# A hybrid S5, attention and mixture-of-experts layer: the beginning ordered by landings, and the attention's roots, rows and outputs moved

## What is computed

```
sh_m, sc_m, g_m, sh_f, sc_f, g_f = split(silu(c) @ w_mod + b_mod, 6)       # and the same with c_ctx
z = (rms_norm(x, g) * (1 + sc_m) + sh_m) @ w_in                            # 2208 columns
mixed = concat(s5(z0), diff_attention(q, k, v), mla(cq, ckv, kr))
x = x + g_m * (mixed @ w_out)
x = x + g_f * moe(modulate(rms_norm(x), sh_f, sc_f))                       # 32 experts, 2 of them per token
# differential attention, 4 heads of 128:
lam = exp(sum(l0 * l1)) - exp(sum(l2 * l3)) + lam_init
p = softmax(q1 k1) - lam * softmax(q2 k2);  o = rms_norm(p @ v, g) * (1 - lam_init)
```

## Time and profile before

| | |
|---|---|
| median of 3 runs | 958.68 us (957.24 to 961.83) |
| the profiled execution's own time | 957.51 us |
| its span, first to last instruction | 955.6 us |
| granted TensorE clock, mean | 0.962 |
| TensorE busy | 866.6 us, 91% |
| VectorE, ScalarE, GpSimd busy | 446.8, 248.4, 134.9 us |
| read from HBM | 264.61 MB |

### The profile page before, as it was taken

The page is one execution under the profiler, slowest core; times in us unless marked ns, Lnnn a source line. Parts: engine busy times, 40 slices in busy tenths (PEclk is TensorE's granted clock), DMA queues, the critical chain, the costliest instruction groups (busy, mean ns, idle before and its releaser), DMA issues.

```text
span 955.6 us, 12764 instructions
## 1 busy us (share of the span) xinstructions
PE 866.6 (91%) x4433; PEld 438.0 (46%) x4433; DVE 446.8 (47%) x1126; ACT 248.4 (26%) x569; POOL 134.9 (14%) x364
## 2 busy tenths in 40 slices
PE   4999999999989989999999999999999976867895
PEld 1675546554445555546534444444444433333232
DVE  4596888769688646025862222222132322212127
ACT  4701023202467564113221111202021211111112
POOL 1311001020100000000011221212121222212110
PEclk9999999999999999999999999999999989787998
DMA  8962203535920373033979999999999999999985
GB/s 338 371 183 37 88 1 113 119 109 218 392 53 1 110 247 128 27 150 144 385 303 385 418 420 418 419 420 420 421 421 418 420 418 418 419 418 418 418 353 227
DMA packets 56374, 267.25 MB, mean 280 GB/s; under 512 B 10838, under 2 KB 17294, under 8 KB 29457
## 3 DMA queue, kind: packets, MB, share of 16 engines
q1 hardware_dynamic: 44432, 249.71, 65.0%
q0 software_dynamic: 11728, 16.99, 6.6%
q10 hardware_dynamic: 176, 0.05, 0.0%
HBM read 264.61 MB, written 25.17 MB: 303 GB/s over the span
## 4 chain that ended last, share of the span: by engine, by line
PE 46%; issue 23%; SPq 11%; DMA 10%; DVE 4%; POOL 3%; ACT 2%; POOLq 1%; ACTq 0%; DVEq 0%
PE PS L803 14%; SPq L413 8%; DMA BIG<-in_moe_w 7%; PE PS L1053 6%; PE PS L984 5%; DMA BIG<-in_w_mod 3%; PE PS L991 2%; PE PS L727 2%; PE PS L1022 2%; POOL held L618 1%; PE PS L1031 1%; SPq L418 1%; POOL BIG L627 1%; PE PS L672 1%; PE PS L1252 1%
## 5 line engine op out<-in xcount | busy, mean ns | idle before, releaser
L803 PE MATMUL PS<-BIG 128*128 128x512 f32 (+2 forms) x352 | 139.5, 553 | 0.0
L803 PEld LDWEIGHTS PS<-BIG 128*128 128x128 f32 x352 | 64.2, 190 | 65.9 <-issue 65.3
L1255 PE MATMUL PS<-S5Z,QKV 128*128 128x512 f32 x192 | 83.4, 592 | 0.0
L1280 PE MATMUL PS<-BIG,GM 128*64 128x512 f32 x320 | 73.6, 601 | 1.5 <-DMA BIG<-in_moe_w 1.5
L1244 PE MATMUL PS<-BIG,QKV 128*32 128x256 f32 x768 | 51.8, 423 | 19.6 <-DMA BIG<-in_moe_w 19.6
L618 POOL TENSOR_TENSOR held<-held 1x1 f32<-1x1 f32 x141 | 25.8, 183 | 301.6 <-PE PS L1228 182.7
L2552 DVE TENSOR_TENSOR QKV<-PS,QKV 64x512 f32<-64x512 f32 x48 | 33.0, 688 | 65.2 <-PE PS L1280 41.0
L1252 PE MATMUL PS<-BIG,QKV 128*64 128x512 f32 x256 | 58.7, 609 | 2.5 <-DMA BIG<-in_moe_w 2.5
L1053 PE MATMUL PS<-BIG 128*128 128x512 f32 x128 | 56.0, 594 | 0.0
L1255 PEld LDWEIGHTS PS<-S5Z,QKV 128*128 128x128 f32 x192 | 36.1, 190 | 43.0 <-issue 43.0
L1633 ACT ACTIVATE QKV<-PS,fcp 128x128 f32<-128x128 f32 x120 | 45.1, 456 | 35.1 <-PE PS L1228 35.1
(11 more groups left out here) (557 smaller groups left out, 1237.3 us busy)
## 6 DMA issues: line engine op xcount, KB each, us to landing
BIG<-in_moe_w SPq DMA_DIRECT2D x84, 1024.0 KB
BIG<-in_moe_w SPq DMA_DIRECT2D x21, 2048.0 KB
S5Z<-in_moe_w SPq DMA_DIRECT2D x40, 1024.0 KB
BIG<-in_w_mod SPq DMA_DIRECT2D x11, 2048.0 KB, 7.6
S5Z<-in_moe_w SPq DMA_DIRECT2D x10, 2048.0 KB, 24.3
BIG<-in_w_in SPq DMA_DIRECT2D x3, 2048.0 KB, 17.7
QKV<-in_x SPq DMA_DIRECT2D x8, 512.0 KB, 10.1
BIG<-in_w_out SPq DMA_DIRECT2D x2, 2048.0 KB, 17.4
```

Source lines behind the costliest of these rows:

```text
L803: ins = mm(dst[:, c0:width], hT[:, k, tok], wslot(n, width)[:, k, c0:width], start=(k == 0), stop=(k == KD - 1))
L1255: ins = mm(bank(2 + m), hgT[:, k, :], w13(side)[:, m, k, :], start=(k == 0), stop=(k == KD - 1))
L1280: ins = mm(PS[64 * n:64 * n + 64, 2560:3072], hidT[:, k % 2, 64 * (k // 2):64 * (k // 2) + 64], w2s(side)[:, k, 512 * n:512 * (n + 1)], st ...
```

## The change

- SP no longer loads c and c_ctx; ScalarE's queue does, ahead of b_mod.
- w_mod's block ("mod", 0, 3) is loaded as two DMAs of 128 rows with a semaphore each; `mod_rows` takes the halves to multiply. The first half's products stand before the tokens' turns, the second's behind. The warm-up products change from 4, 2, 1, 5 to 2, 2, 1, 2 and stand elsewhere.
- Tiles 0 and 1 are modulated slice by slice, each slice signalled by itself, and the first `project_u` takes the slices in the order 0, 4, 1, 5, ... as they come. ScalarE's Sqrt (which loads the table) stands behind `mod_copy(0, 6)`.
- Lambda is computed on two rows instead of 128; a TensorE product with ones spreads the difference.
- `mod_rows(2, 3, 7)`, its turn, copy and columns move into the first blocks of the attention.
- In block 15 ScalarE copies before it takes the exponentials of block 16; head 3's `head_out` goes to block 19, before that block's copy and behind the exponentials of block 20.
- The root of the heads' sums: VectorE makes a first guess by bit operations, and GpSimd three steps of refinement (12 operations on 128x16) that give the inverse root directly. ScalarE's Sqrt and VectorE's reciprocal go.
- `out_part(0, ...)` is split: slice 0 in block 29, slice 1 in block 30, the others in block 31; output 0 uses bank 7.

```diff
+SEED = 0x5F3759DF + (7 << 22)
-        lamr = S5R[:, 0:4 * DHD]
+        lamr = S5R[0:2, 0:2 * DHD]
+        root = S5R[:, 7168 + DH * NLT:7168 + 2 * DH * NLT].bitcast(I32)
+        norm = S5R[:, 7168 + DH * NLT:7168 + 2 * DH * NLT]
+        hT_n = lambda tiles: tiles + 3
+        op_bank = lambda i: 7 if i == 0 else i % 4
...
# SP
-            sp.dma_start(rows[R_C:R_C + 8], a["c"][0].rearrange("(r e) -> r e", e=P)).then_inc(sem("c_in"), 16)
-            sp.dma_start(rows[R_CC:R_CC + 8], a["c_ctx"].rearrange("(r e) -> r e", e=P)).then_inc(sem("c_in"), 16)
+                    if slot_of[n] == RING:
+                        for kk in range(2):
+                            sp.dma_start(mslot(n)[:, kk], src[P * kk:P * (kk + 1)]).then_inc(sem(f"mod_last{kk}"), 16)
+                        continue
# GpSimd
+            pool.wait_ge(sem("ssq"), 1)
+            for again in range(3):
+                st(pool.tensor_tensor(root_tmp, norm, norm, ALU.mult))
+                st.settle()
+                st(pool.tensor_tensor(root_tmp, root_tmp, ssq, ALU.mult))
+                st.settle()
+                st(pool.tensor_scalar(root_tmp, root_tmp, -0.5, 1.5, ALU.mult, ALU.add))
+                st.settle()
+                ins = pool.tensor_tensor(norm, norm, root_tmp, ALU.mult)
...
+            ins.then_inc(sem("rms"), 1)
# TensorE
             mod_rows(0, 0, 6)
+            pe.wait_ge(sem("consts"), 2)
+            warm(2, 1)
...
             mod_rows(0, 1, 6)
-            warm(4, 1)
+            warm(2, 1)
             mod_rows(0, 2, 6)
+            mod_rows(0, 3, 6, (0,))
             for t in range(NCT):
                 turn_tokens(t)
-            warm(2, 1)
-            mod_rows(0, 3, 6)
+            pe.wait_ge(sem("lam"), 3)
+            mm(bank(1, 1, 400), ones[0:2, :], sml[0:2, 492:493], start=True, stop=True).then_inc(sem("lam"), 1)
+            mod_rows(0, 3, 6, (1,))
             warm(1, 1)
             turn_mod(0, 7)
-            warm(5, 1)
+            warm(2, 1)
...
-                for k in range(KD):
+                for k in (0, 4, 1, 5, 2, 6, 3, 7):
+                    if (c, h) == (0, 0):
+                        half, kk = "ad"[k // 4], k % 4
+                        pe.wait_ge(sem(f"hT_{half}"), kk + 1 if kk < 3 else hT_n(NCT))
...
-            mod_rows(2, 3, 7)
             project_latent("nv", 2)
-            turn_mod(2, 7)
...
             for u in range(3):
                 scores(u)
+            mod_rows(2, 3, 7)
...
                 turn_first(b)
+                if b == 1:
+                    turn_mod(2, 7)
...
+                    if t == 0:
+                        pe.wait_ge(sem("b7_free"), len(b7_order))
+                        ring_wait(at[("out", 0)])
+                    if t < 2:
+                        out_part(0, (t,))
                     pe.wait_ge(sem("pt_out"), turned_n(b - 1))
                     pair_values(NHD - 1, slice(t * P, (t + 1) * P))
                 if b == len(blocks) - 1:
-                    out_part(0, range(KD - 1))
+                    out_part(0, range(2, KD - 1))
# ScalarE
+            small(rows[R_C:R_C + 8], vec(a["c"][0], 8), "c_in")
+            small(rows[R_CC:R_CC + 8], vec(a["c_ctx"], 8), "c_in")
             small(rows[R_BMOD:R_BMOD + 48], vec(a["b_mod"][0], 48), "rows_in")
...
+            mod_copy(0, 6)
             A(silu_t[:, 0:1], epsb[:, :], ACT.Sqrt)
-            mod_copy(0, 6)
             act.wait_ge(sem("gmc"), 1)
-            modulated(0)
-            modulated(1)
+            act.wait_ge(sem("xh_tr"), NCT)
+            for k in range(4):
+                for t in range(NCT):
+                    ins = A(hT[:, k, t * P:(t + 1) * P], bank(2 + 2 * t, P, k * P), ACT.Identity,
+                            scale=gmc[:, k, 1:2], bias=modc[:, 8 * M_SH + k, 1:2])
...
-                probs(first_u(b + 1))
+                if b + 1 < NBD:
+                    probs(first_u(b + 1))
+                if b == 0:
+                    mod_copy(2, 7)
                 probs_out(b, 512 * 6, range(4), 2 * b + 1)
+                if b + 1 == NBD:
+                    probs(first_u(b + 1))
...
+                if b - 1 in heads_out and b > NBD:
+                    head_out(heads_out[b - 1])
                 probs_out(b, 512 * 4, range(NT), turned_n(b))
-                if b in heads_out:
-                    head_out(heads_out[b])
-                if b == RMS_AT:
-                    act.wait_ge(sem("ssq"), DH)
-                    A(ssq, ssq, ACT.Sqrt, scale=1.0 / P).then_inc(sem("rms"), 1)
# VectorE
+                if h == DH - 1:
+                    st(ts(root, ssq.bitcast(I32), 1, None, ALU.logical_shift_right))
+                    st(ts(ssq, ssq, 1.0 / P, None, ALU.mult))
+                    st.settle()
+                    ts(root, root, -1.0, float(SEED), ALU.mult, ALU.add).then_inc(sem("ssq"), 1)
...
+                if b == 2:
+                    mod_cols(2, (8, 4), 7, "modc")
...
                 if b == DIAG_AT:
                     dve.wait_ge(sem("rms"), 1)
-                    st(V.reciprocal(ssq, ssq))
```

More of the change, by code:

```diff
@@ L662, in ring_wait, with mod_rows @@
                 pe.wait_ge(sem(f"ring_in{slot_of[n]}"), 16 * sum(slot_of[m] == slot_of[n] for m in range(n + 1)))
-            def mod_rows(g, r, b):
+            def mod_rows(g, r, b, halves=(0, 1)):
                 n = at[("mod", g, r)]
-                ring_wait(n)
-                for kk in range(2):
+                if slot_of[n] != RING:
+                    ring_wait(n)
+                for kk in halves:
                     k = 2 * r + kk
+                    if slot_of[n] == RING:
+                        pe.wait_ge(sem(f"mod_last{kk}"), 16)
                     for j in range(4):
@@ L1846, in _ @@
             dve.wait_ge(sem("gmc"), 1)
-            modulated(0)
-            modulated(1)
+            dve.wait_ge(sem("xh_tr"), NCT)
+            for k in range(4, KD):
+                for t in range(NCT):
+                    ins = ts(hT[:, k, t * P:(t + 1) * P], bank(3 + 2 * t, P, (k - 4) * P),
+                             gmc[:, k, 1:2], modc[:, 8 * M_SH + k, 1:2], ALU.mult, ALU.add)
+                    if k == KD - 1:
+                        ins.then_inc(sem("hT_d"), 1)
+                if k < KD - 1:
+                    ins.then_inc(sem("hT_d"), 1)
             normed(2)
```

67 lines of the change are left out of this document (35 added, 32 removed).

## The result

| | before | changed |
|---|---|---|
| median | 957.96 us (956.59 to 961.83, 4 runs) | 947.21 us (941.78 to 953.16, 4 runs) |
| profiled execution's own time, span | 957.51, 955.6 us | 950.38, 948.3 us |
| granted TensorE clock, mean | 0.962 | 0.966 |
| TensorE busy | 866.6 us | 860.1 us |

A forecast was written before the change was run, and what follows sets the result against it. Bound by TensorE's chain, then from about 500 us by the expert weights' DMA stream. Terms of 2.0, 0.45, 2.2, 5.4 and 0.9 us sum to 10.95, giving 946.6 profiled and 947.8 against the 958.68 median; range 943.5 to 954.0.

The forecast's parts named there:

- beginning: First 60 us: earlier w_mod landings, halved fourth block and slice-wise first projection; gain 2.0 us, bounds 0.2 and 2.6.
- adaLN rows: First attention blocks: moving mod_rows(2,3) behind the third score brings the first turned block 0.45 us earlier; bounds 0 and 1.2.
- block 15: Attention block 15: copying first removes TensorE's 1.12 us wait and keeps the clock; gain 2.2 us, bounds 1.0 and 2.2.
- head 3's copy, roots: Attention blocks 19 to 24: copy's wait, table loads and half clock go; 5.4 us together, 6.3 with fast roots, 4.5 slow.
- out-projection pieces: Last attention blocks: one 0.9 us piece fills one of TensorE's copy waits; gain 0.9 us, bounds 0 and 0.9.
- rival B: Half clock returns in the attention, losing 3.5 us at the roots or 1.1 in block 15; about 951.3 us; chance 0.15.
- What is saved ahead of about 500 us moves the end by as much: Whole kernel: savings on the chain before the full-rate expert weight stream reach the end in full, 10.95 us in sum.
- Rival A: Beginning: c lands late under w_mod's stream, row loads 3 to 4 us later; gain falls to 0.2, 949.6 us; chance 0.15.
- Rival C: Roots: GpSimd's chain beyond 3.3 us after the hand-over holds VectorE; about 960 us at 1.5 us a step; chance 0.02.
- Rival D: Attention savings meet an expert weight load not yet there; only 2 to 3 us pass to the end, 956 us; chance 0.05.
- what the profile after was to show: Signs: first projection near 32, first score about 255.5, turned block 2.5 us earlier, full clock 323 to 365, out-projection near 437.

The follow-up runs named there:

- lam_wide: Changed kernel plus an unused broadcast load of lambda to 128 rows at the old place in GpSimd's queue; 949.09 us, ratio 0.9898.
- c_on_sp: Changed kernel with c and c_ctx loaded by SP ahead of w_mod again; 947.76 us, ratio 0.9899.
- copy_back: Changed kernel with head 3's copy and square behind block 18's own copies again, roots left on GpSimd; 947.15 us, ratio 0.9895.
- block15_back: Changed kernel with block 16's exponentials ahead of block 15's copies again; 950.48 us, ratio 0.9916.
- roots_back: Changed kernel with the square root on ScalarE and the reciprocal on VectorE again, head 3's copy left as changed; 949.42 us, ratio 0.9901.
- begin_only: Kernel before with only the beginning's part of the change, lambda on two rows included; 955.69 us, ratio 0.9972.
- attn_only: Changed kernel with the beginning of the kernel before, attention kept as changed; 951.16 us, ratio 0.9915.
- rows_in_gap: Changed kernel with the product mod_rows(2, 3, 7) alone moved directly behind the last latent projection; 947.17 us, ratio 0.9891.
- rows_back: Changed kernel with mod_rows(2, 3, 7), its turn, copy and columns ahead of the attention again; 946.37 us, ratio 0.9872.

## Why the prediction was right, point by point

| term | predicted | in the profiles | 
|---|---|---|
| beginning | 2.0 | 3.4 |
| adaLN rows | 0.45 | -2.2 |
| block 15 | 2.2 | 3.0 |
| head 3's copy, roots | 5.4 | 7.2 |
| out-projection pieces | 0.9 | 0.9 |
| sum at the out-projection's end | 10.95 | 12.3 |
| between there and the logits' end | 0 | -3.7 |
| between there and the end of the span | 0 | -1.4 |
| sum at the end of the profiled execution | 10.95 | 7.2 |

The time was right (947.8 forecast, 947.21 measured), partly by terms that cancel. That it came within 0.6 us is luck: the four runs span 11.4 us, and all ten runs of the changed kernel have a median of 949.06. For the profiled execution the same sum gave 946.6, and it took 950.38. The two timings of the change gave 10.7 and 8.6 us.

- **Beginning**: the mechanism was right, the size was off. "The 128-fold broadcast of lambda becomes two rows; I count nothing for it" is the step: lam_wide puts it at 1.8 us. What is left, 1.6 us, stands against my 2.0 for c's queue, the halves and the slices; c's queue is 0.5 of it by the third block's start in c_on_sp (0.8 forecast). The four warm-up products that I counted as missing before the third block are not: eight stand ahead of it in both kernels, four of them now ahead of the second.
- **adaLN rows**: this step failed. It said that TensorE "goes on at 260.4 + 1.9 = 262.3", all at full clock, and took 0 as the lower bound. At full clock the move is worth 1.1 us (copy_back); the profile gave back 3.3 us by half clock, which the prediction had put at nothing here, its rival B looking for it only in the later blocks. I had read that the first score comes earlier, and not that taking the product away leaves TensorE idle in the place where it stood, 2.29 us. The product put into the gap avoids this in two of two profiles.
- **Block 15**: 3.0 us, by block15_back 1.3 for the wait and 1.7 for the half clock, against 1.1 and 1.1. A stretch of 3.4 us costs 1.7, half of its length, and I had counted only two scores' stretching.
- **Copy and roots**: GpSimd's twelve steps took 4.1 us (4.6 forecast), VectorE waited 1.00 (1.3 forecast). The parts: 1.2 us for the copy (copy_back; 0.5 forecast), 2.6 for the roots at full clock (roots_back), and 3.4 for the half-clock stretch of 6.8 us that stood in the profile of before. The twelve profiles with at least one of the two edits have no half clock between squares 3 and the pair; the two with neither (before, begin_only) have it, for 6.8 and 3.4 us. With each edit taken back alone the clock stayed full, in one profile each, so each may be enough by itself; why is open.
- **Out-projection pieces**: 0.9, as forecast (from the pair to the out-projection's end 84.10 us for 84.96).
- **"What is saved ahead of about 500 us moves the end by as much"**: true of transfers, as the 413 GB/s from 500 to 930 show, but not of the stretch from 437 to 453. In the profiled run 3.7 us went there, and 1.9 more by the first product of L1296. (The digits of the earlier trace rows turn to 9 for good only in the 22nd slice, from about 502 us; the 21st is a 7.) This is no property of the change: begin_only, whose attention is the old one, has it too, and the kernel before had none under its logits but a stretch at 457 to 460. Of twelve profiles without the added products seven have logits of 12.4 us or more behind the out-projection, five 9.1 to 9.6; of two with them none has.
- **Rival A** (949.6): c came at 6.95 and the first silu_c at 8.02, as it said, and the loss did not follow, as c_on_sp shows: TensorE has to wait for the first w_mod block too, in the changed kernel until 8.66. The Trainium skill, DMA: Bandwidth & Descriptors, section "Queues, rings and completion order", would have a small load wait for packets of a large one; the 4.2 us of delay, of which 0.2 is the later issue, agree with it.
- **Rival B** (951.3): no half clock in blocks 15 to 26, so it did not happen where I put it; it happened at the first scores and in the router instead, with 3.3 and 3.7 us. **Rival C**: the steps were 0.30 us apart, two of them longer (0.41 and 0.61). Those two lie beside VectorE's scalings at 342.75 and 344.37, and each ends 0.07 us behind the scaling. This agrees with the Trainium skill, SBUF — State Buffer, section "SBUF: two separate sides", and cost 0.6 us of the 1.2 at most. C's 960 us for 1.5 us a step comes to 961.2 by its own sum. **Rival D** (956): ruled out at medians, 947.21 and 949.06 for the whole and 951.16 for attn_only alone.
- **Of what the profile after was to show** the first projection (31.09), the waits gone in block 15 and near 350, GpSimd's steps, the clock from 323 to 365 and the out-projection (435.4 for "near 437") came out. The first score came at 254.17 for 255.5, and the turned block 1.2 us earlier instead of 2.5.

Still open: what decides, in one and the same code, between a full and a half clock at the first scores (copy_back against the changed kernel) and in the router (rows_in_gap against rows_back). Filling TensorE there changed how often it occurred in these profiles; no experiment set it on or off at will, and the whole times did not tell the versions apart.

## What to carry to other kernels

Count what a small transfer takes from the stream beside it by the time of its packets and not by its bytes: 131 KB spread from one row to 128 held up the weights by 1.7 us, where its bytes would take 0.3. What makes its packets slow (the one source row, the small rows, GpSimd's queue) was not separated. When a product is moved away from where the next stage is not ready, it leaves an idle stretch; that stretch is a place for it, which in two of two profiles kept the clock full. Judge an edit of 1 to 3 us by distances between two landmarks in the trace, with the granted clock beside them; whole times of this kernel, 941.8 to 953.2 us in ten runs of one code, do not resolve it.

## What the runs showed of the hardware

- Half clock comes in places that have nothing to do with the edit. Behind the 2.29 us of idle ahead of the first scores 7 of 9 profiles had it, and both profiles of the changed kernel had 13.66 us of it in the router. A stretch cost about half of its length where TensorE was on the chain (1.7 us of 3.4 in block 15, 3.3 and 3.4 of 6.8 at the first scores and at the roots), and less in the router, 3.7 us of 13.7 up to the logits' end.
- An idle stretch ahead is not enough to explain it: 2.76 us of waiting in roots_back was followed by full clock, and the wait of 1.1 us in block 15 by half clock in the kernel before and in block15_back and by full clock in begin_only.
- GpSimd's 128x16 operations took 0.20 to 0.22 us and followed one another in 0.30, except two of 0.41 and 0.61 us beside VectorE's scalings.
- A load of 128 rows of 1 KB from one source row cost the 424 GB/s stream beside it 1.7 us: its 32 packets of 4096 bytes took 0.78 us each, the weights' of 8192 bytes 0.32.
- The changed kernel scatters more than the one before: a standard deviation of 3.9 us over its ten runs, 2.1 over all 42 of the kernel before.
